# Laying weight panels out in DRAM as they lie in SBUF, in a four-layer diffusion trunk

## The chip, the core and the metric

The kernel runs on one core of a Trainium2 chip. The metric is the time of one execution on the device in microseconds (us), 1892.81 us for the kernel before (median of three runs). Engines are called PE (TensorE, matrix products), DVE (VectorE), ACT (ScalarE), POOL (GpSimd) and SP (SyncE, which only issues transfers here). Transfers between DRAM and the on-chip memory SBUF are done by 16 DMA engines, fed by queues: q1 is SP's, q10 is ACT's, q0 is POOL's.

## The reference

384 tokens of width 1024 (128 context, 256 latent) pass four layers. Each layer is a mixer and a mixture of experts, both modulated by vectors that come from `silu(cond) @ w_ada`:

```python
for i in range(DEPTH):                       # DEPTH = 4
    kind, j = i % 3, i // 3                  # 0 attention, 1 pooling, 2 retention
    mp = split(silu(c_ctx) @ w_ada[i] + b_ada[i], 6)      # w_ada: (4, 1024, 6144)
    ms = split(silu(c) @ w_ada[i] + b_ada[i], 6)
    h = rmsnorm(x) * norm1 * (1 + scale) + shift
    y = mixer(h)     # attn_w_qkv (1024, 1536), attn_w_o (1024, 1024); pool_w (4, 256, 256);
                     # ret_w_in (1024, 6144), ret_w_out (2048, 1024)
    x = x + gate * y
    h = rmsnorm(x) * norm2 * (1 + scale2) + shift2
    x = x + gate2 * moe(h)                   # 16 experts, two of them per token
y = rmsnorm(x) * norm_f
```

The retention mixer splits `h @ ret_w_in` into q and k (8 heads of 128), v and a gate (8 heads of 256), runs a forward and a backward scan over chunks of 128 tokens, and multiplies by `ret_w_out`. All values are float32.

## The kernel before

Weights of the mixers and of the modulation reach SBUF in **panels**: `panel` (line 112) is four buffers of 8 x 512 values per partition, 16 KB per partition, 2 MB each. A panel holds 1024 rows of a weight, row `k * 128 + p` at block k of partition p, and up to 512 columns. `load_panel` (line 307) issues it from SP; `panel_source` (314), `ret_qkv_source` (329) and `ret_gate_source` (334) say which part of the weight it is. The weights lie in DRAM as in the reference, so a partition's data is 8 pieces, one from each k, and the pieces are whole row parts:

- 64 modulation panels, 384 columns wide: 48 of them (layers 0 to 2) are loaded from line 372 (`load_ada`) before and during the attention of layer 0, alternating between panel buffers 2 and 3; 16 (layer 3) from line 380 (`load_ret_ada`) inside the retention loop. A piece is 1.5 KB.
- for each of the two attention layers (0 and 3) three panels of `attn_w_qkv` and two of `attn_w_o`, 512 columns wide, pieces of 2 KB.
- one pooling panel (layer 1), 256 columns wide in a 512-wide buffer.
- for each of the 8 heads of layer 2 a panel with q, k and v, put together by three transfers (pieces of 512 B, 512 B and 1 KB), and a gate panel of 256 columns (1 KB).
- four panels of `ret_w_out`, 512 columns wide: two for each half of the output columns.

All of these but the modulation panels alternate between buffers 0 and 1. A buffer is loaded again when PE has signalled that it has read it (`released`, line 244). For `ret_w_out` that is the end of a half of the output columns, after which the last two panels are loaded.

The experts' weights go through the same memory in other shapes (`load_half`, `load_down`, lines 343 to 350), in pieces of 4 KB; their layout is not touched.

**Between layers.** When PE has finished the experts of a layer it signals `experts_read` (line 1018), on which SP loads the first panels of the next layer (line 409): the pooling panel before layer 1; q/k/v and gate of head 0 and two modulation panels before layer 2; two `attn_w_qkv` panels before layer 3. In layers 1 and 3 the first experts' weights follow behind them in SP's queue. At the same time ACT stores the last experts' output rows to a DRAM table `y_by_slot`, and when they have landed POOL issues six indirect gathers (line 1857), two for each tile of 128 tokens, 128 rows of 4 KB each. ACT weights a landed pair (line 1800), DVE combines and gates it (lines 1472 and 1474), and POOL (first two tiles, line 1861) or DVE (last tile, line 1479) adds it to x. ACT squares and sums x, POOL takes the root, ACT scales x to `xn` (line 1568), and PE transposes it (line 512). PE has nothing else to do meanwhile.

In layer 0 PE weaves the modulation products (`pe_static_product`, line 552, matmuls at line 564) between the steps of the attention, one panel at a time. In layer 2 the loop over heads in `pe_retention` (line 723) does projections (lines 757 and 768), the scan, and two modulation products per head (line 541).

## Time and profile before

| | |
|---|---|
| median of 3 runs | 1892.81 us (1890.38 to 1894.35) |
| profiled execution | 1892.95 us, span 1890.8 us |
| PE busy | 1536.1 us, 81% |
| DVE, ACT, POOL busy | 521.1, 432.1, 130.9 us |
| mean granted PE clock | 0.911 of full speed |
| DMA | 196,042 packets, 436.91 MB, 231 GB/s over the span |
| SP's queue q1 | 179,504 packets, 392.75 MB, 56.7% of the 16 engines' time |

The profile is that of one execution. Its page gives busy times, groups of instructions by line, and counts by DMA queue. The list of waits tells how long an engine stood idle before an instruction and what released it; the timeline lists instructions with their start; the table by stage gives busy times, the granted clock, the share of time in which the 16 DMA engines were busy (it can pass 1, since the records of packets overlap a little) and what they moved. A share of the 16 engines' time divided by the number of packets gives what one packet takes of one engine. Packets of 4 bytes, with which transfers signal their end, are among the counts.

The busy share of the DMA engines is near 1 where the experts' weights are loaded and in the opening, 0.90 during most of layer 0's attention, and 0.46 in the retention loop.

### The profile page before, as it was taken

The page shows a single profiled execution, that of the slowest core. Times are in us where ns is not written, and L with a number is a line of the kernel's source. Part 1 is how long each engine was busy: PE and PEld are TensorE (multiplying, and loading weights), DVE is VectorE, ACT ScalarE, POOL GpSimd, SP SyncE. Part 2 cuts the span into 40 slices and gives each one's busy share as a digit, 9 for nine tenths or more (in the row PEclk, how much of TensorE's full clock was granted, in tenths as well). Part 3 has the DMA queues.
Part 4 walks back from the last instruction along what each step waited for, and adds up shares of the span by engine and source line. Part 5 has one row for each costly group of instructions (what it writes and reads, how often), then busy time and mean ns, then how long its engine had stood idle before and what let it go on. Part 6 is the DMA issues. An engine that isn't in the chain of part 4 may idle for free. (4 is left out here: it accounts for less than half of the span.)

```text
span 1890.8 us, 19158 instructions
## 1 busy us (share of the span) xinstructions
PE 1536.1 (81%) x7307; PEld 843.5 (45%) x7307; DVE 521.1 (28%) x1292; ACT 432.1 (23%) x836; POOL 130.9 (7%) x113
## 2 busy tenths in 40 slices
PE   5998779699835899299999998986997498969952
PEld 3445444444334444165555555434443347444421
DVE  0323100432037421332222222005410355063103
ACT  2114220312143111341111111003111306131211
POOL 0000001200023000200000000002000100110002
PEclk7999989899968899699999999897999699979976
DMA  9777886679863599634444444053897721039993
GB/s 358 246 274 254 309 305 211 266 298 411 329 258 111 210 412 398 214 104 148 147 144 144 144 146 165 0 222 134 330 412 305 291 89 51 0 134 380 412 364 112
DMA packets 196042, 436.91 MB, mean 231 GB/s; under 512 B 9552, under 2 KB 114800, under 8 KB 195824
## 3 DMA queue, kind: packets, MB, share of 16 engines
q1 hardware_dynamic: 179504, 392.75, 56.7%
q10 hardware_dynamic: 12992, 30.40, 4.3%
q0 software_dynamic: 3456, 12.58, 1.8%
q8 instruction: 54, 0.88, 0.2%
q14 instruction: 36, 0.29, 0.0%
HBM read 410.00 MB, written 25.69 MB: 230 GB/s over the span
## 5 line engine op out<-in xcount | busy, mean ns | idle before, releaser
L888 PE MATMUL bank<-gate_up_weights,hT_gathered 128*64 128x512 f32 (+1 forms) x1280 | 258.3, 605 | 23.4 <-SPq L478 20.0
L757 PE MATMUL bank<-panel,hT 128*128 128x512 f32 x384 | 170.5, 598 | 0.7 <-ACT mod_bc L1587 0.7
L888 PEld LDWEIGHTS bank<-gate_up_weights,hT_gathered 128*64 128x64 f32 (+1 forms) x1280 | 84.1, 134 | 189.7 <-issue 185.5
L512 PE MATMUL bank<-const_base,xn 128*128 128x128 f32 x192 | 39.3, 395 | 132.0 <-ACT xn L1568 132.0
L902 PE MATMUL bank<-down_weights,actT 128*64 128x512 f32 (+1 forms) x640 | 138.5, 603 | 2.3 <-ACT actT L1766 2.3
L584 PE MATMUL bank<-panel,hT 128*128 128x512 f32 x288 | 126.1, 595 | 1.1 <-DVE hT L1084 1.1
L564 PE MATMUL bank<-panel,cond_columns 128*32 128x384 f32 x768 | 86.6, 576 | 31.5 <-DMA panel<-in_w_ada 26.9
L757 PEld LDWEIGHTS bank<-panel,hT 128*128 128x128 f32 x384 | 71.2, 190 | 90.9 <-issue 90.1
L873 PE MATMUL bank<-h_hi,P 128*128 128x512 f32 x216 | 95.9, 444 | 9.8 <-DVE P L1417 9.8
L512 PEld LDWEIGHTS bank<-const_base,xn 128*128 128x128 f32 x192 | 37.1, 214 | 136.8 <-issue 115.1
L1593 ACT ACTIVATE ada_panel_rows<-bank 128x384 f32<-128x384 f32 x64 | 31.4, 490 | 270.8 <-PE bank L564 155.7
L873 PE MATMUL bank<-h_lo,P 128*128 128x512 f32 x216 | 88.9, 412 | 0.0
L584 PEld LDWEIGHTS bank<-panel,hT 128*128 128x128 f32 x288 | 53.9, 190 | 70.4 <-issue 69.1
L584 PE MATMUL bank<-panel,oT 128*128 128x512 f32 x192 | 84.2, 596 | 0.7 <-ACT oT L1673 0.7
L1456 DVE TENSOR_TENSOR act<-bank,silu 128x256 f32<-128x256 f32 x36 | 15.3, 424 | 251.5 <-ACT silu L1760 251.5
L768 PE MATMUL bank<-panel,hT 128*128 128x256 f32 x384 | 84.2, 379 | 0.0
L1099 DVE TENSOR_TENSOR residual_term<-bank,gate_bc 128x512 f32<-128x512 f32 x24 | 16.5, 691 | 229.3 <-PE bank L834 93.0
L768 PEld LDWEIGHTS bank<-panel,hT 128*128 128x128 f32 x384 | 72.4, 190 | 10.0 <-issue 0.5
L1771 ACT ACTIVATE y_rows<-bank 128x512 f32<-128x512 f32 x72 | 43.0, 597 | 139.6 <-PE bank L902 139.6
L1760 ACT ACTIVATE silu<-bank 128x256 f32<-128x256 f32 x36 | 13.8, 385 | 255.3 <-PE bank L888 255.3
L1857 POOL DMA_INDIRECT y_of_token<-y_by_slot,slot_of_token x24 | 22.9, 955 | 650.3 <-DMA y_by_slot<-y_rows 644.2
L873 PEld LDWEIGHTS bank<-h_hi,P 128*128 128x128 f32 x216 | 43.4, 201 | 43.7 <-issue 28.8
(269 smaller groups left out, 1999.7 us busy)
## 6 DMA issues: line engine op xcount, KB each, us to landing
panel<-in_w_ada SPq DMA_DIRECT2D x64, 1536.0 KB
down_weights<-in_moe_w_down SPq DMA_DIRECT2D x74, 1024.0 KB, 15.2
gate_up_weights<-in_moe_w_gate SPq DMA_DIRECT2D x148, 512.0 KB, 13.2
gate_up_weights<-in_moe_w_up SPq DMA_DIRECT2D x148, 512.0 KB, 14.2
y_by_slot<-y_rows ACTq DMA_DIRECT2D x36, 512.0 KB, 7.1
panel<-in_ret_w_in SPq DMA_DIRECT2D x16, 1024.0 KB
panel<-in_attn_w_qkv SPq DMA_DIRECT2D x6, 2048.0 KB
panel<-in_attn_w_o SPq DMA_DIRECT2D x4, 2048.0 KB
```

What stands on the lines that cost most here:

```text
L512: last = PE.transpose(ps[k % 4][:, t * 128:(t + 1) * 128], xn[:, t, k * 128:(k + 1) * 128], ident)
L564: last = PE.matmul(ps[7][32 * g:32 * g + 32, 0:ADA_N], cond32[:, 2 * g + kk, :], src[:, 2 * g + kk, 0:ADA_N], start=kk == 0, stop=kk == 1)
L584: last = PE.matmul(ps[bank][:], lhs(k, t), panel[s % 2][:, k, :], start=k == 0, stop=k == nk - 1)
L757: last = PE.matmul(ps[t][:], hT[:, k, t * 128:(t + 1) * 128], panel[f % 2][:, k, :], start=k == 0, stop=k == KD - 1)
L768: last = PE.matmul(ps[3 + t // 2][:, (t % 2) * 256:(t % 2) * 256 + 256], hT[:, k, t * 128:(t + 1) * 128], panel[(f + 1) % 2][:, k, 0:256], ...
L873: last = PE.matmul(ps[half][:], Pm[:, j, t, :], part[:, t, half * 512:half * 512 + 512], start=t == 0 and n == 0, stop=t == TILES - 1 and ...
L888: last = PE.matmul(ps[2][width * s:width * s + width, :], hg[:, j, k, width * s:width * s + width], gu_ring[w][:, :, k, :], start=k == 0, ...
L902: last = PE.matmul(ps[6 + half][width * s:width * s + width, :], actT[:, c, width * s:width * s + width], dn_ring[w][:, c, half * 512:half ...
L1099: V.tensor_tensor(tmp[:, m % 2, :], ps[3 * half + t][:], gate_bc[:, COND[t], half * 512:half * 512 + 512], ALU.mult).then_inc(sem("mix_ter ...
L1593: S.activation(mpan[:], ps[bank][:, 0:ADA_N], ACT.Copy).then_inc(sem("ada_evac"), 1)
L1771: S.activation(ybuf[:, par, half * 512:half * 512 + 512], ps[6 + half][:], ACT.Copy).then_inc(sem("row_y"), 1)
L1857: G.indirect_dma_start(ytok[:, a, t, :], None, y_rows[:], bass.IndirectOffsetOnAxis(slot_of_token[:, a, t:t + 1], 0)).then_inc(sem(f"y_gat ...
```

## The change

The host writes new arrays, in which every panel lies as its buffer does: for each of the 128 partitions the 8 pieces one behind the other (12 KB for a modulation panel, 16 KB for one of 512 columns, 8 KB for one of 256), and the partitions in order, so that a panel is one contiguous block of DRAM. The q, k and v columns of a retention head are put side by side, so that its panel is one transfer instead of three. The sources in the kernel are changed to these arrays. The buffers in SBUF, their number, the order of all transfers, the semaphores and what every engine computes stay the same. Modulation panels still fill 384 of the 512 columns of a buffer row, gate and pooling panels 256 of 512.

```diff
+def panel_layouts(inputs):
+
+    def columns(w, n):
+        *lead, rows, cols = w.shape
+        w = w.reshape(*lead, rows // 128, 128, cols // n, n)
+        w = np.moveaxis(w, (-2, -3, -4), (len(lead), len(lead) + 1, len(lead) + 2))
+        return np.ascontiguousarray(w).reshape(*lead, cols // n, 128, rows // 128 * n)
...
+    q, k, v, g = np.split(w["ret_w_in"][0], (RH * RK, 2 * RH * RK, 2 * RH * RK + RH * RV), axis=1)
+    heads = np.concatenate([q.reshape(D, RH, RK), k.reshape(D, RH, RK), v.reshape(D, RH, RV)], axis=2).reshape(D, RH * 512)
...
-    ada_w = A["w_ada"].rearrange("l (k p) n -> l p k n", p=128)
-    qkv_w = A["attn_w_qkv"].rearrange("l (k p) n -> l p k n", p=128)
...
+    ada_w, qkv_w, wo_w = A["ada_panels"], A["qkv_panels"], A["wo_panels"]
+    rin_w, rgate_w, rout_w, pool_w = A["ret_panels"], A["ret_gate_panels"], A["rout_panels"], A["pool_panels"]
...
+        rows = lambda w, n: w.rearrange("p (k n) -> p k n", n=n)
         if kind == "ada":
-            return lambda d: [(d[:, :, 0:ADA_N], ada_w[l, :, :, ds(i * ADA_N, ADA_N)])]
-        if kind == "attn" and not isinstance(i, int) or kind == "attn" and i < 3:
-            return lambda d: [(d[:, :, :], qkv_w[a, :, :, i * 512:(i + 1) * 512])]
+            src = ada_w[l, i] if isinstance(i, int) else ada_w[l, ds(i, 1)].rearrange("o p c -> (o p) c")
+            return lambda d: [(d[:, :, 0:ADA_N], rows(src, ADA_N))]
+        if kind == "attn" and i < 3:
+            return lambda d: [(d[:, :, :], rows(qkv_w[a, i], 512))]
...
     def ret_qkv_source(h):
-        return lambda d: [(d[:, :, 0:RK], rin_w[0, :, :, ds(h * RK, RK)]),
-                          (d[:, :, RK:2 * RK], rin_w[0, :, :, ds(h * RK + RH * RK, RK)]),
-                          (d[:, :, 2 * RK:512], rin_w[0, :, :, ds(h * RV + 2 * RH * RK, RV)])]
+        return lambda d: [(d[:, :, :], of_head(rin_w, h, 512))]
 
     def ret_gate_source(h):
-        return lambda d: [(d[:, :, 0:RV], rin_w[0, :, :, ds(h * RV + 2 * RH * RK + RH * RV, RV)])]
+        return lambda d: [(d[:, :, 0:RV], of_head(rgate_w, h, RV))]
```

## Rows read from the trace of the kernel before

**Rows 1.** Waits of PE, whole span: what waited, released by: us, times, longest us.
```profile
PE bank L512 <- ACT xn L1568: 132.0, 8, 36.4
PE bank L564 <- DMA panel<-in_w_ada: 26.9, 19, 2.7
```

**Rows 2.** Timeline, layer 2: first matmuls on the third `ret_w_out` panel.
```profile
1241.52 2.08 PE L834 MATMUL bank<-panel,yT_even 128*128 128x512 f32 x2 [7.98 <-DMA panel<-in_ret_w_out]
```

**Rows 3.** Waits of PE in 814 to 1190 us, the retention loop; the longest group.
```profile
PE bank L783 <- DVE ret_q_bwd L1238: 10.5, 8, 1.3
```

**Rows 4.** Table by stage: stretch, its us, engines busy; then PE clock, DMA share, GB/s.
```profile
28.00:34.00 6.00, 3.33 (x22) 1.69 (x22) 0.46 (x3) 2.83 (x6) 1.66 (x3) 0.50 1.06 373
180.00:288.00 108.00, 83.27 (x648) 49.40 (x639) 12.82 (x41) 26.84 (x70) 0.00 (x0) 0.87 0.90 310
665.00:705.00 40.00, 40.00 (x190) 18.16 (x188) 9.82 (x24) 9.06 (x18) 0.00 (x0) 1.00 1.03 412
766.00:769.00 3.00, 0.00 (x0) 0.00 (x0) 0.00 (x0) 0.00 (x0) 1.93 (x2) 0.50 1.03 292
814.00:1180.00 366.00, 339.48 (x1412) 210.21 (x1412) 85.03 (x242) 68.96 (x131) 6.56 (x8) 1.00 0.46 147
1480.00:1482.00 2.00, 0.00 (x0) 0.00 (x0) 1.33 (x1) 1.67 (x3) 2.00 (x1) 0.50 1.05 386
```

**Rows 5.** DMA queues (packets, MB, share): whole span; 817.5 to 823; 852 to 854.5.
```profile
q8 instruction: 54, 0.88, 0.2%
...
q10 hardware_dynamic: 148, 0.95, 41.3%
...
q10 hardware_dynamic: 158, 0.15, 17.3%
```

**Rows 6.** Waits of PE in 150 to 290 us, the attention of layer 0.
```profile
PE bank L564 <- DMA panel<-in_w_ada: 22.3, 15, 2.7
```

**Rows 7.** Timeline from layer 2 to layer 3: SP, POOL, ACT, DVE, PE.
```profile
1461.53 1.02 POOL L1857 DMA_INDIRECT y_of_token<-y_by_slot,slot_of_token  x1 [155.16 <-DMA y_by_slot<-y_rows]
1462.93 1.03 SPq L312 DMA_DIRECT2D panel<-in_attn_w_qkv  x2
1479.48 1.15 ACT L1800 ACTIVATE y_of_token<-y_of_token,route_scratch 128x1024 f32<-128x1024 f32 x1 [2.99 <-DMA y_of_token<-y_by_slot,slot_of_token]
1480.67 2.70 DVE L1472 SCALAR_TENSOR_TENSOR y_of_token<-y_of_token,route_scratch 128x1024 f32<-128x1024 f32 x1 [0.80 <-ACT y_of_token L1800]
1484.66 1.23 DVE L1479 TENSOR_TENSOR x<-x,y_of_token 128x1024 f32<-128x1024 f32 x1
1490.67 4.68 PE L512 MATMUL bank<-const_base,xn 128*128 128x128 f32 x24 [33.42 <-ACT xn L1568]
```

**Rows 8.** DMA queues in 529 to 534, 774 to 781.5, 1467.5 to 1478 us.
```profile
q1 hardware_dynamic: 287, 1.04, 51.5%
q0 software_dynamic: 287, 1.04, 51.3%
...
q0 software_dynamic: 634, 2.32, 77.9%
q1 hardware_dynamic: 677, 0.68, 25.8%
...
q0 software_dynamic: 694, 2.52, 60.4%
q1 hardware_dynamic: 857, 1.72, 42.8%
```

**Rows 9.** DMA queues in 1465.8 to 1467.5 us.
```profile
q1 hardware_dynamic: 278, 0.57, 88.7%
q0 software_dynamic: 25, 0.09, 14.7%
```

**Rows 10.** From layer 1 to layer 2: SP's issues, POOL's first gather; queue q0 in 766 to 771.
```profile
764.05 4.72 SPq L312 DMA_DIRECT2D panel<-in_ret_w_in  x4
766.62 0.99 POOL L1857 DMA_INDIRECT y_of_token<-y_by_slot,slot_of_token  x1 [155.27 <-DMA y_by_slot<-y_rows]
...
q0 software_dynamic: 4, 0.02, 0.9%
```

More of the change, by code:

```diff
@@ L85, in shape_constants @@
     return {"k_base": base, "k_ret": ret, "k_rope": rope, "k_cnt": (np.float32(1) / cnt)}
+def panel_layouts(inputs):
[4 more added lines that the diff above has]
+        return np.ascontiguousarray(w).reshape(*lead, cols // n, 128, rows // 128 * n)
+    w = {n: np.asarray(inputs[n]) for n in ("w_ada", "attn_w_qkv", "attn_w_o", "pool_w", "ret_w_in", "ret_w_out")}
+    q, k, v, g = np.split(w["ret_w_in"][0], (RH * RK, 2 * RH * RK, 2 * RH * RK + RH * RV), axis=1)
+    heads = np.concatenate([q.reshape(D, RH, RK), k.reshape(D, RH, RK), v.reshape(D, RH, RV)], axis=2).reshape(D, RH * 512)
+    out = columns(w["ret_w_out"][0].reshape(2, D, D), 512)
+    pools = w["pool_w"].reshape(-1, KD, 128, 256).transpose(0, 2, 1, 3).reshape(-1, 128, KD * 256)
+    return {"ada_panels": columns(w["w_ada"], ADA_N), "qkv_panels": columns(w["attn_w_qkv"], 512), "wo_panels": columns(w["attn_w_o"], 512),
+            "ret_panels": columns(heads, 512), "ret_gate_panels": columns(g, RV), "pool_panels": np.ascontiguousarray(pools),
+            "rout_panels": np.ascontiguousarray(out.transpose(1, 0, 2, 3)).reshape(4, 128, KD * 512)}
 def build_trunk(nc, A, O, depth=DEPTH):
@@ L259, in panel_landed @@
         eng.wait_ge(sem(f"panel_landed{s % 2}"), 48 * (s // 2 + 1) + i * (48 * per // 2))
-    ada_w = A["w_ada"].rearrange("l (k p) n -> l p k n", p=128)
-    qkv_w = A["attn_w_qkv"].rearrange("l (k p) n -> l p k n", p=128)
-    wo_w = A["attn_w_o"].rearrange("l (k p) n -> l p k n", p=128)
-    rin_w = A["ret_w_in"].rearrange("l (k p) n -> l p k n", p=128)
-    rout_w = A["ret_w_out"].rearrange("l (k p) n -> l p k n", p=128)
+    ada_w, qkv_w, wo_w = A["ada_panels"], A["qkv_panels"], A["wo_panels"]
+    rin_w, rgate_w, rout_w, pool_w = A["ret_panels"], A["ret_gate_panels"], A["rout_panels"], A["pool_panels"]
     wg_w = A["moe_w_gate"].rearrange("l e (p k) f -> l e p k f", p=128)
@@ L315, in panel_source, with of_head @@
         a = l // 3
+        rows = lambda w, n: w.rearrange("p (k n) -> p k n", n=n)
         if kind == "ada":
[L317 to L319 removed]
+            src = ada_w[l, i] if isinstance(i, int) else ada_w[l, ds(i, 1)].rearrange("o p c -> (o p) c")
+            return lambda d: [(d[:, :, 0:ADA_N], rows(src, ADA_N))]
+        if kind == "attn" and i < 3:
+            return lambda d: [(d[:, :, :], rows(qkv_w[a, i], 512))]
         if kind == "attn":
[L321 removed]
+            return lambda d: [(d[:, :, :], rows(wo_w[a, i - 3], 512))]
         if kind == "pool":
[L323 to L324 removed]
+            return lambda d: [(d[:, :, 0:256], rows(pool_w[a], 256))]
         if kind == "rout":
[L326 removed]
+            return lambda d: [(d[:, :, :], rows(rout_w[i], 512))]
         raise ValueError(kind)
+    def of_head(w, h, n):
+        src = w[h] if isinstance(h, int) else w[ds(h, 1)].rearrange("o p c -> (o p) c")
+        return src.rearrange("p (k n) -> p k n", n=n)
     def ret_qkv_source(h):
[L330 to L332 removed]
+        return lambda d: [(d[:, :, :], of_head(rin_w, h, 512))]
     def ret_gate_source(h):
[L335 removed]
+        return lambda d: [(d[:, :, 0:RV], of_head(rgate_w, h, RV))]
     def at_e(w, l, e):
@@ L1893, in build_trunk @@
     ctx.close()
-_INS = ["x_prompt", "x_sample", "cache_k", "cache_v", "state_ret", "w_ada", "b_ada", "attn_w_qkv", "attn_q_norm",
-        "attn_k_norm", "attn_w_o", "pool_w", "ret_w_in", "ret_decay_logit", "ret_norm", "ret_w_out",
+_INS = ["x_prompt", "x_sample", "cache_k", "cache_v", "state_ret", "b_ada", "attn_q_norm",
+        "attn_k_norm", "ret_decay_logit", "ret_norm",
         "moe_w_gate", "moe_w_up", "moe_w_down"]
@@ L1917 @@
     arrays["router"] = np.concatenate([weights.reshape(128, -1), np.broadcast_to(bias, (128, bias.size))], axis=1).astype(np.float32)
+    arrays.update(panel_layouts(inputs))
     arrays.update(shape_constants())
```

4 lines of the change are left out of this document (removed).

## The prediction, made before the changed kernel ran

> **What bounds the kernel now.** I read the page first: TensorE (PE) is busy for 81% of the span, so the question is what ends its idle time, and whether a panel is ever the last thing to arrive. The waits of PE answer it [rows 1]. The largest item, 132.0 us in 8 waits, is PE standing idle at the norms until ScalarE has written `xn`; between layers that is the combine of the experts' outputs (store to DRAM, gather back by token, weight, add), not a panel. Panels from `w_ada` end 26.9 us in 19 waits, and one panel of `ret_w_out` ends one of 7.98 us [rows 2]; no other panel ends any. Inside the retention loop no wait is put down to a DMA; the longest group waits for DVE, 10.5 us in 8 [rows 3]. So of the 95 panels only the modulation panels of layer 0 and one output panel of layer 2 can give time by landing sooner.
>
> Then I asked what a panel costs the 16 DMA engines. Stretches in which one packet size has the engines to itself give the rate: runs of 1.5 KB move 373 GB/s, of 2 KB 386, of 4 KB 412, and the retention panels (512 B and 1 KB mixed) 292 [rows 4]. Per engine (16 x bytes / rate) that is 65.9 ns for 1.5 KB, 84.9 for 2 KB and 159 for 4 KB. The last two give a line of 10.8 ns + 36.2 ns per KB; it puts 1.5 KB at 65 ns, so a packet pays a fixed 11 ns and the rest is bytes. No stretch shows a separate toll for scattered rows: 1.5 KB rows fetched 24 KB apart lie on the line of the experts' 4 KB runs. That is why I expect nothing from locality itself. The Trainium skill (DMA: Bandwidth & Descriptors, section on latency and other measured facts) warns that DRAM row pitches of large powers of two can halve the rate, and the old `ret_w_out` and `attn_w_o` panels do step by 512 KB from one k to the next. [...]
>
> **What the change does to each panel.** I count a packet as long as the shorter of its two contiguous runs, in DRAM and in SBUF. Panels that fill a 512-wide buffer (`attn_w_qkv`, `attn_w_o`, `ret_w_out`, the q, k, v of a head) become contiguous on both sides: 128 packets of 16 KB in place of 1024 of 2 KB, or 3072 of 512 B and 1 KB. Packets above 4 KB do exist unsplit: the instruction queue has 54 in 0.88 MB, 16 KB each, and the 8 KB rows of `ret_norm` take 313 ns of an engine each (0.413 x 5.5 us x 16 / 116, the line gives 301) [rows 5]. By the line a 16 KB packet takes 604 ns, 434 GB/s; 412 GB/s is the lower bound. The modulation (1.5 KB of a 2 KB row), gate and pooling panels (1 KB of 2 KB) are still written in short pieces in SBUF. The nearest row for a transfer whose one side is longer than the other is the store of `ret_state_out`: 2 KB contiguous in SBUF, 1 KB runs in DRAM. It shows 158 packets for 0.15 MB, so 1 KB each, at about 48 ns, no cheaper than a 1 KB packet on the line (47) [rows 5]. I take it that these panels keep their packets and their price.
>
> **Part 1, modulation panels of layer 0: 0 us.** In 180 to 288 us the DMA engines are 90% busy [rows 4], with 1.5 KB packets, and from 150 to 290 PE waits 22.3 us for panels in 15 waits [rows 6]. This is the place where faster panels would pay. With the packets unchanged it pays nothing. Bounds: no loss, since the experts' weights, contiguous by partition like the new panels, run at 412 GB/s [rows 4]; at the other end the gain of the second rival below.
>
> **Part 2, the output panel of layer 2: -0.5 us.** SyncE may issue the third `ret_w_out` panel only when half 0 is done, and PE resumes at 1241.52 after 7.98 us [rows 2]. 2.10 MB at 386 GB/s are 5.43 us, at 434 GB/s 4.83, at 412 5.09: 0.3 to 0.6 saved, the latency stays. Behind it PE has three tiles of 16 matmuls before it needs the fourth panel, so nothing else is late.
>
> **Part 3, retention and attention panels elsewhere: 0 us.** Their landings are covered: PE waits for DVE and ACT in the loop [rows 3], where the DMA engines are 46% busy [rows 4]. SyncE issues one transfer per head where it issued three; its queue holds nothing that PE awaits. What their cover costs if it is gone: one landing, 5 us, at each head.
>
> **Part 4, the gather between layers 2 and 3: +5.9 us.** Here a panel costs time without anyone waiting for it. GpSimd issues six gathers of 512 KB from 1461.53, and SyncE, released by the same end of the experts, issues two `attn_w_qkv` panels (4.19 MB) from 1462.93 [rows 7]. Both use the same 16 engines, the gathers as queue q0, SyncE's loads as q1. How these are shared shows where the two queues run side by side, in counts: 287 packets against 287 when both are 4 KB, 634 against 677 when the other side is 1 KB, 694 against 857 at 2 KB [rows 8] (4-byte ones included). So the engines alternate packet by packet, whatever their size. With 1 or 2 KB opposite, the gather had two thirds or more; with 16 KB opposite it has 4 of 20. Worked out: from 1467.5 to 1478 the gather moves its last 2.52 of 3.15 MB [rows 8], in the 1.7 us before 0.09 (a gap in which q1 has the engines) [rows 9], so 0.54 by 1465.8. After the change q1 has about 0.9 MB through at 1467.5 (1.7 us at 434 GB/s and the little before), which leaves 3.3 MB or 202 packets of 16 KB. A pair, 604 + 159 ns, over 16 engines is 21 pairs per us: 9.6 us, to 1477.1, in which the gather moves 202 x 4 KB = 0.83 MB and stands at 1.44 of 3.15. The rest goes against the experts' 4 KB packets at the measured 1.04 MB per 5 us: 8.2 us, to 1485.3 instead of 1478, +7.3. The path behind it: the third weighting (L1800) would start at 1486.8 instead of 1479.48; then 1.15 + 1.28 + 1.22 + 1.23 us and hand-overs bring the last add to 1491.8, against 1485.89. Before, L1472 took 2.70 beside GpSimd's add [rows 7]; a later one has no such neighbour, which returns 1.4. PE's norm waits for exactly this chain: +5.9. Bounds: 0 if the gather's share does not fall, +7.8 if the panels drain first (third rival).
>
> **Part 5, the same between layers 1 and 2: +0.5 us.** SyncE issues at 764.05, GpSimd at 766.62, and the gather's data starts only after 771 (0.02 MB in 766 to 771) [rows 10]. 2.10 MB in 16 KB packets from about 766 are through at 771; then come gate and modulation panels, as before. 0 to 1.8 us (three packets of 604 ns ahead of a late store or a first gather packet); I take 0.5, near the lower end since the overlap is nearly nil. Between layers 0 and 1 the pooling panel keeps 1 KB packets: 0.
>
> **Sum.** 0 - 0.5 + 0 + 5.9 + 0.5 = +5.9 us. The profiled execution lasted 1892.95 us, its span 1890.8; the median of three is 1892.81, 0.14 less. 1892.81 + 5.9 = **1898.7 us**.
>
> **Rivals.** First, *no difference*: 16 KB runs are cut into pieces of about 4 KB, or the engines alternate in smaller units than what the trace calls a packet. Then the gather has half: 2.52 MB at 0.208 MB per us are 12.1 us instead of 10.5, so at most +1.6. Against it: the unsplit 8 KB rows. Result 1892.3 to 1894.5. That covers also a change that does not do what it says.
>
> Second, *faster*: the price of a packet sits on the DRAM side. Then a modulation panel, now read in 12 KB runs, costs 3.82 us (412 GB/s) instead of 4.22, 0.40 less. In 15 waits that is 6.0 us, with the opening's six panels 2.4 more; the granted clock in 180 to 288 is 0.87 after these pauses and 1.00 in the retention loop [rows 4], and of the 83.3 us that PE is busy there up to 0.13 x 83.3 = 10.8 could go, of which I count 6 at most. Gain 8.4 to 14.4, less the 5.9 of the sum: 1884.3 to 1890.3, centre 1887. It wins from about 15 cheaper panels on. For it: the two sides of a transfer may well be cut separately; the Trainium skill (same page, section on semaphore increments) mentions loads on this chip whose reads are widened over several rows. Against it: the state store.
>
> Third, *worse*: in 1465.8 to 1467.5 the gather got 25 packets against 278 [rows 9]. If this is a backlog that drains first, all 16 KB packets go first, to 1475.0, then 2.54 MB at 0.208 MB per us: 1487.2, +7.8 on the path, and 1.8 at the boundary before: 1901.9.
>
> **Numbers.** Forecast 0.45, no difference 0.17, faster panels 0.25, drained first 0.10, other 0.03. The range from 1884 to 1902 leaves out the lower tail of the second rival and the upper of the third. A difference of 0.2% (3.8 us) is about what can be told from none. Slower: 0.40 of the forecast's 0.45, plus the third: 0.50. Same: 0.05 + 0.17 + 0.09 (where gain and loss cancel): 0.31. Faster: 0.16 + 0.03: 0.19.
>
> **What would show it.** In the profile after: fewer packets in all, about 196,000 less 36,000; 1.5 KB stretches still at 373 GB/s (rival two: 400 or more); in the gather before layer 3 about as many q0 as q1 packets, and the idle time of PE ahead of L512 there 39 us instead of 33.4; the wait for `ret_w_out` 7.5 us. The prediction is wrong if SyncE issues the layer 3 panels some us earlier than the gather, as it does before layer 2, since most of their bytes would then be gone before the two meet.

## The result, and the profile of the changed kernel

The changed kernel took 1906.03 us (median of 4 runs, 1901.09 to 1907.83), the kernel before 1893.58 us beside it: a ratio of 1.0064, 95% interval 1.0044 to 1.0083, so it is slower by 12.5 us. The direction is as forecast, and so is one place of the loss, the gather before layer 3. The size is not: +5.9 us were predicted, and the time lies above the upper end of the range (1902). A second set of runs of the same kernel on another chip gave a ratio of 1.0107 (1.0078 to 1.0136).

The page of the changed kernel (packets in all; then the queues, with packets, MB and share of 16 engines):

```profile
DMA packets 159690, 436.91 MB, mean 230 GB/s; under 512 B 9296, under 2 KB 89968, under 8 KB 156656
...
q1 hardware_dynamic: 143152, 392.75, 56.1%
q10 hardware_dynamic: 12992, 30.40, 4.2%
q0 software_dynamic: 3456, 12.58, 1.8%
```

The waits of PE over the whole span (released by: us, times, longest us):

```profile
PE bank L530 <- ACT xn L1586: 137.2, 8, 40.2
PE bank L582 <- DMA panel<-in_ada_panels: 27.3, 18, 3.6
PE bank L801 <- DVE ret_q_bwd L1256: 10.5, 8, 1.3
PE bank L852 <- DMA panel<-in_rout_panels: 7.8, 1, 7.8
PE bank L906 <- DMA gate_up_weights<-in_moe_w_up: 5.6, 5, 1.7
```

L530 is the old L512, L582 the old L564, L801 the old L783, L852 the old L834 and L906 the old L888. Against [rows 1] the idle time before the norms has grown by 5.2 us, and its longest piece from 36.4 to 40.2. The waits for modulation panels are where they were (26.9 before). The last line has no counterpart in the kernel before: PE now waits for the experts' weights, which the change does not touch. That line is the first trace of what the prediction missed.

The table by stage (stretch, its us, engines busy, then PE clock, DMA share, GB/s):

```profile
28.00:34.00 6.00, 3.33 (x19) 1.91 (x22) 0.46 (x3) 3.06 (x6) 1.65 (x3) 0.50 1.06 373
180.00:288.00 108.00, 83.61 (x632) 51.31 (x631) 12.82 (x41) 27.28 (x70) 0.00 (x0) 0.86 0.90 306
665.00:705.00 40.00, 40.00 (x192) 18.17 (x188) 9.82 (x24) 8.99 (x18) 0.00 (x0) 1.00 1.02 404
814.00:1180.00 366.00, 339.34 (x1413) 209.98 (x1412) 84.66 (x240) 69.75 (x132) 5.96 (x7) 1.00 0.43 147
```

Beside [rows 4]: the 1.5 KB stretch still runs at 373 GB/s, the attention of layer 0 still has the DMA engines about 90% busy (306 GB/s where it had 310), and in the retention loop PE is as busy as before, with the DMA engines at 43% instead of 46%. The experts' stretch, 665 to 705, has gone from 412 to 404 GB/s at a nearly unchanged share of busy engines (1.02 and 1.03).

To see where the time went I cut both profiled executions at three marks in each layer: GpSimd's first `h_lo` (the router), GpSimd's first gather, and PE's first matmul of the next norm. Times in us:

| stretch | before | after | difference |
|---|---|---|---|
| start to layer 0's router | 359.2 | 356.6 | -2.6 |
| experts, layers 0, 1, 2 | 160.6, 161.0, 160.7 | 164.4, 164.0, 165.0 | +11.1 |
| gather to norm, layers 0 to 1, 1 to 2 | 32.0, 29.6 | 31.5, 28.7 | -1.4 |
| gather to norm, layers 2 to 3 | 29.1 | 35.8 | +6.7 |
| mixer of layer 1 | 53.8 | 53.3 | -0.5 |
| mixer of layer 2 | 504.6 | 500.5 | -4.1 |
| mixer, experts and end of layer 3 | 400.1 | 399.2 | -0.9 |

The sum is +8.3, against +8.1 between the spans of 1898.9 and 1890.8 us (the marks are rounded). This profiled execution, 1901.09 us, is the fastest of the four. Mixer 2 is 500 to 506 us long in the runs below, old layout or new, so I read nothing into its 4 us. Two items remain: the gather before layer 3, as forecast, and the experts' stages, which no term of the sum had.

The gather before layer 3. Timeline from layer 2 to layer 3:

```profile
1463.81 1.02 POOL L1875 DMA_INDIRECT y_of_token<-y_by_slot,slot_of_token  x1 [159.31 <-DMA y_by_slot<-y_rows]
1464.93 2.85 SPq L327 DMA_DIRECT2D panel<-in_qkv_panels  x2
...
1476.78 1.15 ACT L1818 ACTIVATE y_of_token<-y_of_token,route_scratch 128x1024 f32<-128x1024 f32 x1 [16.73 <-DMA y_of_token<-y_by_slot,slot_of_token]
...
1484.80 1.15 ACT L1818 ACTIVATE y_of_token<-y_of_token,route_scratch 128x1024 f32<-128x1024 f32 x1 [6.87 <-DMA y_of_token<-y_by_slot,slot_of_token]
...
1489.86 1.15 ACT L1818 ACTIVATE y_of_token<-y_of_token,route_scratch 128x1024 f32<-128x1024 f32 x1 [3.92 <-DMA y_of_token<-y_by_slot,slot_of_token]
...
1499.63 0.66 PE L530 MATMUL bank<-const_base,xn 128*128 128x128 f32 x2 [40.24 <-ACT xn L1586]
```

The queues in 1469.8 to 1480.3 us (packets, MB, share), the stretch that lies as far behind the first gather as the last one of [rows 8]:

```profile
q1 hardware_dynamic: 270, 3.35, 75.2%
q0 software_dynamic: 269, 1.02, 23.7%
```

270 packets against 269, with q1's panels in 16 KB packets and q0 in 4 KB ones: one for one, so the gather moves 1.02 MB where it had moved 2.52 [rows 8]. The third weighting starts 26.05 us after the first gather; it was 17.95 [rows 7].

The experts. The end of layer 0's experts on PE in the changed kernel:

```profile
500.04 3.64 PE L906 MATMUL bank<-gate_up_weights,hT_gathered 128*32 128x512 f32 x32
505.41 3.64 PE L906 MATMUL bank<-gate_up_weights,hT_gathered 128*32 128x512 f32 x32 [1.74 <-DMA gate_up_weights<-in_moe_w_up]
510.02 0.44 PE L912 MATMUL bank<-const_base,act 128*128 128x128 f32 x2 [0.97 <-DVE act L1474]
511.33 5.34 PE L920 MATMUL bank<-down_weights,actT 128*32 128x512 f32 x32 [0.88 <-ACT actT L1784]
```

and the same in the kernel before:

```profile
502.88 7.07 PE L888 MATMUL bank<-gate_up_weights,hT_gathered 128*32 128x512 f32 x64
510.92 0.44 PE L894 MATMUL bank<-const_base,act 128*128 128x128 f32 x2 [0.96 <-DVE act L1456]
511.83 3.64 PE L902 MATMUL bank<-down_weights,actT 128*32 128x512 f32 x32 [0.47 <-ACT actT L1766]
```

Before, the 64 gate and up matmuls ran through. After, PE stops for 1.74 us in the middle for an `in_moe_w_up` half, and the 32 down matmuls behind the pause then take 5.34 us instead of 3.64. The granted clock of 500 to 518 us is 0.91 in the changed kernel, so part of it ran at the lower level of 1.2 GHz (511 to 514 us, right behind the two pauses, has 0.58), and 1.00, 2.4 GHz throughout, in the kernel before. The changed kernel's row:

```profile
500.00:518.00 18.00, 13.06 (x98) 3.86 (x98) 0.42 (x1) 2.55 (x5) 0.00 (x0) 0.91 0.42 164
```

So this late weight was paid twice. The cause of the lateness had to be sought. While the experts' weights are loaded the DMA engines are fully busy in both kernels (665 to 705 us above), and the change edits none of these loads. What it does change for them is where their arrays stand in the order in which the inputs are declared. The change replaces six arrays ahead of the experts' three by seven behind them.

### The profile page after: what moved, and what is told of

It reads as the page before. It is cut to its first block and busy times, and to the rows that moved or that the text cites. A ratio compares the mean times of both kernels' runs of the same rounds, so it can differ in the third digit from the quotient of the medians.

```text
span 1898.9 us, 19114 instructions
## 1 busy us (share of the span) xinstructions
PE 1529.6 (81%) x7307; PEld 837.6 (44%) x7307; DVE 519.0 (27%) x1292; ACT 430.8 (23%) x836; POOL 131.3 (7%) x113
## 5 line engine op out<-in xcount | busy, mean ns | idle before, releaser
L906 PE MATMUL bank<-gate_up_weights,hT_gathered 128*64 128x512 f32 (+1 forms) x1280 | 256.4, 599 | 30.3 <-SPq L496 21.3
L906 PEld LDWEIGHTS bank<-gate_up_weights,hT_gathered 128*64 128x64 f32 (+1 forms) x1280 | 83.3, 132 | 195.7 <-issue 181.9
L530 PE MATMUL bank<-const_base,xn 128*128 128x128 f32 x192 | 36.1, 372 | 137.2 <-ACT xn L1586 137.2
L582 PE MATMUL bank<-panel,cond_columns 128*32 128x384 f32 x768 | 84.9, 566 | 31.7 <-DMA panel<-in_ada_panels 27.3
L891 PE MATMUL bank<-h_hi,P 128*128 128x512 f32 x216 | 95.3, 441 | 11.1 <-DVE P L1435 11.1
L530 PEld LDWEIGHTS bank<-const_base,xn 128*128 128x128 f32 x192 | 33.9, 201 | 142.4 <-issue 120.2
L920 PEld LDWEIGHTS bank<-down_weights,actT 128*64 128x64 f32 (+1 forms) x640 | 36.3, 134 | 65.2 <-issue 57.3
## 6 DMA issues: line engine op xcount, KB each, us to landing
gate_up_weights<-in_moe_w_gate SPq DMA_DIRECT2D x148, 512.0 KB, 13.6
gate_up_weights<-in_moe_w_up SPq DMA_DIRECT2D x148, 512.0 KB, 14.9
```

The costliest lines, as they stand in the source:

```text
L530: last = PE.transpose(ps[k % 4][:, t * 128:(t + 1) * 128], xn[:, t, k * 128:(k + 1) * 128], ident)
L582: last = PE.matmul(ps[7][32 * g:32 * g + 32, 0:ADA_N], cond32[:, 2 * g + kk, :], src[:, 2 * g + kk, 0:ADA_N], start=kk == 0, stop=kk == 1)
L891: last = PE.matmul(ps[half][:], Pm[:, j, t, :], part[:, t, half * 512:half * 512 + 512], start=t == 0 and n == 0, stop=t == TILES - 1 and ...
L906: last = PE.matmul(ps[2][width * s:width * s + width, :], hg[:, j, k, width * s:width * s + width], gu_ring[w][:, :, k, :], start=k == 0, ...
L920: last = PE.matmul(ps[6 + half][width * s:width * s + width, :], actT[:, c, width * s:width * s + width], dn_ring[w][:, c, half * 512:half ...
```

## Experiments

"Stages" are the experts' stretches of layers 0 to 2 as cut above, "gaps" the three stretches from gather to norm. Times in the verdicts are medians; each ratio is to the kernel before on the same chip.

**Theories.** G: the gather is starved by 16 KB packets, and this is all. P: the order of the arrays costs something by itself. L: the new panels themselves slow later loads. The first four runs separate them.

**The order alone.** The kernel before, with the six arrays declared behind the others:

```diff
+    for n in ("w_ada", "attn_w_qkv", "attn_w_o", "ret_w_in", "pool_w", "ret_w_out"):
+        arrays[n] = arrays.pop(n)
     arrays.update(shape_constants())
```

> The kernel before, with its old layouts, but the six weight arrays declared last among the DRAM inputs, where the changed kernel has its panel arrays (same sizes). Theory P (the order of the arrays in DRAM slows the experts' weight loads, which cost 3 to 4 us in each of the first three layers of the changed kernel): 1899 us or more against 1893, with pauses of PE for gate_up weights in the last row of each layer. Theory G (only the 16 KB packets opposite the gather cost time) and theory L (the new panels themselves slow later loads): 1893, within 2 us.

Measured: 1897.28 us, ratio 1.0038 (1.0019 to 1.0057); stages 164.3, 162.7, 162.3; gap before layer 3 28.6. Three waits of PE for `in_moe_w_up`, 1.8 us. Not one transfer is different, and 7 us are lost; the three stages together are 7.0 us longer. Theory G alone falls.

**The changed kernel in the old order.** The seven new arrays take the places of the six old ones:

```diff
+    order = ["x_prompt", "x_sample", "cache_k", "cache_v", "state_ret", "ada_panels", "b_ada", "qkv_panels", ..., "moe_w_gate", "moe_w_up", "moe_w_down", "vectors", "router"]
+    arrays = {n: arrays[n] for n in order + [n for n in arrays if n not in order]}
```

> The changed kernel, with its arrays declared in the order of the kernel before, so that the experts' weights stand where they stood. Theory P: 6 us less than the changed kernel, near 1899, and PE waits of L906 for gate_up weights gone. Theories G and L: 1905, as the changed kernel.

Measured: 1898.82 us, ratio 1.0057 (1.0038 to 1.0075). Stages 160.3, 161.1, 161.2, no wait for the experts' weights, gap before layer 3 35.9. The experts' loss is cured with all the new panels in place, so theory L falls; the gather's stays. But the time is still 10.8 us above the kernel before (7.2 to 14.2), 4 to 5 us more than the gather explains, and the start to the first router takes 364.4 us, where the kernel before has 359.2.

**Two panels alone.** The kernel before with only the first two `attn_w_qkv` panels of layer 3 laid out by the host, in an array behind all others:

```diff
+        if kind == "attn" and l == 3 and i < 2:
+            return lambda d: [(d[:, :, :], A["two_panels"][i].rearrange("p (k n) -> p k n", n=512))]
```

> The kernel before, with only the first two attn_w_qkv panels of layer 3 contiguous (16 KB packets), as one further array at the end. Theory G: PE's idle time before the norm of layer 3 rises from 33.4 to 39 to 41 us and the time by 6 to 7 us, to 1899.5. If the 16 KB packets do not matter there: 1893 and 33.4 us.

Measured: 1893.95 us, ratio 1.0029 (1.0007 to 1.005), 5.5 us. PE's idle time before the norm of layer 3 is 40.3 us and the gap 36.0, the changed kernel's values, from 2 of 95 panels. Stages 160.3, 160.9, 160.2.

**Those two undone.** The changed kernel, with these two panels read from the old layout (a copy of it at the end of the arrays):

```diff
+        if kind == "attn" and l == 3 and i < 2:
+            return lambda d: [(d[:, :, :], A["attn_w_qkv"].rearrange("l (k p) n -> l p k n", p=128)[a, :, :, i * 512:(i + 1) * 512])]
```

> The changed kernel, with only these two panels of layer 3 loaded in the old layout (2 KB packets) from a copy of the old array at the end. Theory G: the idle time before the norm of layer 3 is back to 33 to 34 us and the time 6 to 7 us below the changed kernel, near 1899; what then remains over 1893 is not the gather's. If the gather is not the cause: 1905.

Measured: 1900.02 us, ratio 1.0058 (1.0037 to 1.0079). Gap 28.8, idle time 33.5: the gather's loss is gone, yet the kernel is still 11 us slower than the one before (7.0 to 14.9), hardly less than the changed kernel itself. The waits for the experts' weights are there (1.3 us in 2), and the stages are 161.1, 162.4 and 163.0, 4.2 us more than before in sum. The start to the first router is long again, 365.5 us.

**The changed kernel again**, on the chip of the next three:

> The changed kernel again, unchanged, beside the others of this group. Gather (about +7) and array order (about +7) together: 12 to 14 us over the kernel before. In its trace the gap from the first gather to the norm of layer 3 is 36 us and each of the first three experts' stages 162 to 165 us, against 29 and 161 before.

Measured: 1909.93 us, ratio 1.0107 (1.0078 to 1.0136); gap before layer 3 35.4, three waits for `in_moe_w_up`, 3.1 us. Stages 161.0, 161.8, 164.6: only the third is as long as was expected, so the loss by the order varies from one execution to the next.

**The gather has the engines to itself.** The kernel before, with SyncE held back until the gathers of the layer have landed:

```diff
                 sp.wait_ge(sem("experts_read"), l)
+                for t in range(TILES):
+                    sp.wait_ge(sem(f"y_gathered{t}"), 32 * l)
```

> The kernel before, but SyncE waits for the six gathers of a layer before it issues the next layer's first panels, so that the gather has the DMA engines to itself. If sharing the engines is what makes the gather long even with 2 KB packets: the gap from the first gather to the norm falls from 32.0, 29.6 and 29.1 us to about 24 each (alone, at the end of the kernel, the third pair is weighted 12.8 us after the first gather, against 17 to 22 in the middle), so 15 to 20 us less in all, near 1872 where the kernel before has 1889. If the loads, now 10 to 13 us late, are then waited for, the gain is given back: PE would pause for panels or gate_up weights.

Measured: 1879.51 us, ratio 0.9939 (0.9918 to 0.9959). Timeline before layer 3:

```profile
1457.36 1.02 POOL L1859 DMA_INDIRECT y_of_token<-y_by_slot,slot_of_token  x1 [155.36 <-DMA y_by_slot<-y_rows]
...
1469.88 1.15 ACT L1802 ACTIVATE y_of_token<-y_of_token,route_scratch 128x1024 f32<-128x1024 f32 x1 [1.66 <-DMA y_of_token<-y_by_slot,slot_of_token]
1470.03 1.03 SPq L312 DMA_DIRECT2D panel<-in_attn_w_qkv  x2
```

The third weighting starts 12.5 us after the first gather, where the kernel before has 17.95 and the changed one 26.05. The three gaps are 25.9, 25.8 and 25.4 us, 13.6 less in sum; mixer 1 gives 1.9 back because its panels come later (55.7 in place of 53.8). The difference, 11.7, agrees with the gain measured, 11 us, though the profiled execution is the slowest of the nine (span 1882.9 against 1890.8, with 2.5 us more in the start). The gather was being slowed before the change too, only less.

**Shorter packets' price.** The kernel before, where only the modulation panels are laid out by the host and are packed in their SBUF buffer as well, so that both sides of the transfer are runs of 12 KB (the matmuls read the packed view):

```diff
+            whole = lambda d: d[:].rearrange("p k n -> p (k n)")[:, 0:KD * ADA_N]
+            return lambda d: [(whole(d), src)]
```

> The kernel before, with only the modulation panels laid out by the host, and also packed in their SBUF buffers (8 x 384 values without gaps), so that both sides are contiguous: 128 packets of 12 KB per panel. If the short run in SBUF is what kept the packets of the changed kernel at 1.5 KB: 57,000 packets fewer, a panel costs about 3.6 us of the engines instead of 4.2, and PE's waits for modulation panels (27 us) fall to 15 to 20, the time by 6 to 12 us. If the packet price does not matter there: 1889, as before.

Measured: 1885.67 us, ratio 0.9978 (0.9954 to 1.0002), 4 us, an interval that just includes no gain. The page and the table by stage:

```profile
DMA packets 138698, 436.91 MB, mean 232 GB/s; under 512 B 9552, under 2 KB 49264, under 8 KB 130288
...
28.00:34.00 6.00, 3.81 (x26) 1.50 (x30) 0.15 (x1) 1.09 (x3) 0.93 (x2) 0.63 0.98 394
```

57,344 packets fewer from 64 panels, and the opening runs at 394 GB/s instead of 373. In the changed kernel the same panels, contiguous in DRAM, kept their 1.5 KB packets and the 373 GB/s. So in these transfers a packet is as long as the shorter run of the two sides.

**The experts' arrays first of all**, in the kernel before (six arrays and the small ones behind them):

> The kernel before, with the three arrays of experts' weights declared first among the DRAM inputs and nothing else changed. If the order of the old kernel was a lucky one and most others are slower: experts' stages of 162 to 165 us and 1893 to 1897. If only the new order is unlucky: 161 us each and 1889.

Measured: 1888.34 us, ratio 0.999 (0.9974 to 1.0005), stages 160.4, 160.7, 161.5. It is not that the experts' arrays begin early in DRAM.

**The wait in the changed kernel.** The three lines of the gather's wait added to it, order of arrays as changed:

> The changed kernel, whole, in its own order of arrays, with SyncE held back until the gathers of the layer before have landed, so that no 16 KB packet meets a gather. If the gather's starvation is worth what the idle of PE before the norms shows (40 us before layer 3 down to 30, 36 and 33 down to 30 before layers 1 and 2, 19 us in all): about 1890 to 1893, that is 0 to +3 us against the kernel before, since what the order of the arrays costs (5 to 7 us) and the longer experts' stages stay. Rival, the late panels are now waited for: the norms' idle falls but PE waits for the first qkv and modulation panels afterwards, 5 us each, and the time stays at 1900 or more. Second rival, the starvation explains all of the change's cost and the array order nothing: 1880, like the kernel before with the same wait.

Measured: 1891.66 us, ratio 1.0019 (1.0002 to 1.0035); gaps 25.7, 25.6, 26.5; stages 162.2, 165.4, 162.1; four waits for `in_moe_w_up`, 2.8 us. The gather's part is gone, and what the stages lose is the order's. The total does not close: the order's 7 to 9 us less the 11 us of the wait would be 2 to 4 us faster than the kernel before, and it is 3.6 slower.

**All layouts, old order, packed modulation panels, and the wait** (the changed kernel with all three edits):

> All of the host layouts, the arrays declared in the order of the kernel before, the modulation panels packed in their buffer too (12 KB packets), and SyncE held back until the gathers have landed. If the costs of the change are the gather's starvation and the array order and nothing else, both are gone: as fast as the kernel before with the same wait (11 us under the kernel before) and the 0 to 5 us of the packed modulation panels on top: 1875 to 1881. If there is a third cost of the 16 KB packets (in the experts' stages or in the retention layer), it shows as a time above 1881, with experts' stages above 161 us or the stage of mixer 2 above 505 us.

Measured: 1872.83 us, ratio 0.9921 (0.99 to 0.9942); stages 160.1, 161.0, 160.8; start to router 353.2.

**Packed modulation panels and the wait alone**, every other panel and array as before:

> The kernel before with two edits: modulation panels laid out by the host and packed in their buffer (12 KB packets), and SyncE held back until the gathers have landed. No other panel is changed, no array moved. The two gains add if they are separate (11 and 4 us): 1875 to 1880. Against the run with all panels laid out: equal if 16 KB packets of the other panels neither help nor harm once the gather is alone; below it if they harm elsewhere; above it by up to 2 us if the retention and attention panels gain. Only the 11 us if the packed modulation panels bring nothing: 1880 to 1882.

Measured: 1872.97 us, ratio 0.9921 (0.9903 to 0.9938); start to router 351.1. Both are 15 us faster than the kernel before and equal to each other within their intervals of some 4 us: no gain or harm of the attention, output, retention and pooling layouts is seen once the gather is alone and the order is the old one. The gains of the wait (11 us) and of the packed panels (4 us) add up to what is measured; the times themselves lie below the ones expected because the kernel before took 1887.71 us on this chip.

**The order alone, again**, with more runs:

> The kernel before with the six weight arrays declared last, the same as in the earlier run, in more rounds, because the earlier interval (+3.6 to +10.8 us) rests on few runs. If the order of arrays in DRAM costs time by itself: +4 to +10 us again, experts' stages of layers 0 to 2 at 162 to 164 us in place of 161, and waits of PE in the gate/up lines put down to DMA. If the earlier result was a difference between loadings of a program and not of the order: within 3 us of the kernel before, experts' stages 160 to 161.

Measured: 1896.17 us, ratio 1.0041 (1.0026 to 1.0056), stages 162.7, 164.9, 162.6.

**Which array's place?** In the kernel before, `w_ada` alone last:

> The kernel before with only w_ada (101 MB) declared last. If it is w_ada's place behind the experts' arrays that costs time (its panels are fetched beside the experts' weights in every layer): +5 to +9 us, experts' stages of layers 0 to 2 at 162 to 165 us. If it is the place of the other five, or only where the experts' arrays begin when all six are gone: within 3 us, stages at 160 to 161.

Measured: 1887.25 us, ratio 0.9996 (0.9984 to 1.0008), stages 160.4, 161.1, 161.4. The other five last:

> The kernel before with the five other weight arrays (attn_w_qkv, attn_w_o, ret_w_in, pool_w, ret_w_out; 56 MB) declared last and w_ada in place. If w_ada's place is the cause: within 3 us of the kernel before. If any shift of the experts' arrays to a start that differs from the old one costs time: +5 to +9 us.

Measured: 1897.22 us, ratio 1.0046 (1.0027 to 1.0066), stages 164.6, 164.4, 162.2. All six last, and the experts' arrays first of all:

> The kernel before with the six arrays last and the experts' arrays first of all: as in the run with the six last, w_ada lies behind the experts' arrays, but the 4.3 MB of small arrays (x, caches, state, b_ada) lie between them. If what costs is that w_ada lies behind the experts' arrays: +5 to +9 us. If it is the experts' start behind the 4.3 MB of small arrays: within 3 us, as in the run with the experts' arrays first.

Measured: 1888.31 us, ratio 1.0001 (0.9984 to 1.0018), stages 160.2, 161.0, 160.2. Neither `w_ada`'s place nor the amount of weight ahead of the experts decides. If the arrays lie one behind the other as declared, the experts' arrays begin at 153 MiB in the kernel before, at 57 with `w_ada` last and at 0 when first, none of which costs; at 4 MiB with the six last and at 100 with the five last, which cost (all but the 0 plus the same 0.1 MiB of small arrays). The costly ones are even, the harmless ones odd or exactly 0, and the only one of the six whose size is an odd number of MiB is `pool_w`, 1 MiB. This gave the last pair.

**`pool_w` alone last:**

```diff
+    for n in ("pool_w",):
+        arrays[n] = arrays.pop(n)
```

> The kernel before with pool_w alone (1.05 MB, the smallest weight array) declared last, so that everything declared after it moves by 1 MiB, the experts' arrays with it. If an odd shift of the experts' arrays by 1 MiB is what costs: +6 to +9 us, experts' stages of layers 0 to 2 at 162 to 165 us, from moving one small array. If the amount of weight ahead of the experts' arrays, or the place of one of the large ones (qkv, o, ret_w_in, ret_w_out), is what costs: within 3 us, stages at 160 to 161.

Measured: 1898.85 us, ratio 1.0046 (1.003 to 1.0062), stages 161.2, 162.6, 162.8, two waits for `in_moe_w_up`. The sum of the stages is 4.3 us above the kernel before, and so is the span of this execution, the fastest of the twelve.

**All but `pool_w` last:**

> The kernel before with five weight arrays (w_ada, qkv, o, ret_w_in, ret_w_out; 155 MB) declared last and pool_w left in its place. It moves almost all that the costly order moves, but the experts' arrays by an even number of MiB (148). If the shift by 1 MiB costs: within 3 us of the kernel before, stages at 160 to 161. If the place of the large arrays costs: +6 to +9 us.

Measured: 1892.43 us, ratio 1.0006 (0.999 to 1.0023), stages 160.1, 161.0, 162.2. The table by stage for 1730 to 1790 us (layer 3's experts), `pool_w` last:

```profile
1730.00:1790.00 60.00, 60.00 (x286) 26.52 (x284) 14.00 (x36) 12.20 (x24) 0.00 (x0) 1.00 1.02 402
```

and all but `pool_w` last:

```profile
1730.00:1790.00 60.00, 60.00 (x286) 26.49 (x284) 12.23 (x30) 12.21 (x24) 0.00 (x0) 1.00 1.02 411
```

To move one array of 1 MiB, which is read in 1 of 95 panels, costs 8 us; to move 148 MiB and leave that one costs nothing that can be measured. (In layer 3, whose experts' stretch from router to gather is longer, 184 us, the lower rate costs no time: it is 184.1 in both.) What the DMA engines show is more slow packets. The usual 4 KB packet takes 159 ns; those over 200 ns, counted from router to gather in all four layers, are 1635 with `pool_w` last, 1308 with all but `pool_w` last and 1148 in the kernel before. Over all twenty traces of this study, the twelve in which the experts' arrays begin at an odd MiB or at 0 have 1045 to 1308 such packets, and the eight in which they begin at an even one 1405 to 1651. A short stretch does not separate them so well: in 390 to 500 us it is 115 to 237 against 261 to 320, but in 1725 to 1795 us 14 to 120 against 99 to 192, which overlap.

**The order in the changed kernel**, with the gather's wait, to be set beside the same kernel in the new order (1.0019):

> The changed kernel with SyncE held back until the gathers have landed and its arrays declared in the old order; the run in the new order was 4 us slower than the kernel before (1.0019). If the order costs 7 us in the changed kernel too: 3 to 4 us faster than the kernel before, or more, up to 11 faster (the whole gain of the wait), with experts' stages at 161 us. If the order costs nothing in the changed kernel: +4 us again. The packed modulation panels of the fastest runs are not in this one, so what it lacks of -15 us is theirs.

Measured: 1886.73 us, ratio 0.9984 (0.9968 to 1.0), stages 160.4, 160.6, 160.8, no wait for the experts' weights. The order is worth 0.35%, some 7 us, here too.

This kernel and the one with all layouts (0.9921) differ in one thing, whether the modulation panels are packed in their buffer. That is 12 us, each taken against the kernel before on its own chip, and in the profiled executions the start to the first router alone is longer by that much, 365.8 against 353.2 us (spans 1883.5 and 1873.5). In the kernel before, laying out and packing the same panels gave 4 us together. So laid out and not packed, as the change has them, they seem to cost some 8 us against the old layout. No run has them alone, so this is a difference of ratios and not shown by itself.

## Why the prediction was right about the gather and wrong in its sum

The step that failed is the sum. It has no term for the experts' stages, which is to put them at 0 without a reason, and the runs showed 7 to 9 us there, from the order of the arrays alone. The gather's mechanism held and its term was about right. Variants of the changed kernel show a further loss of 2 to 9 us, whose cause stays open.

**Part 1, modulation panels: 0 forecast, borne out by the profiled execution, not by all runs.** 15 waits of 23.0 us in 150 to 290 us against 22.3 [rows 6], and packets and the rate of the opening are unchanged, as taken from the shorter run. But in three of six kernels with these panels the start is 5 to 7 us longer than in the kernel before (see what stays open), so 0 may be wrong. The second rival (the price sits on the DRAM side) is refuted by the unchanged 373 GB/s and, from the other side, by the packed run, where the SBUF side alone made the difference. Its gain was sized too high: with really cheaper packets the start is 6 to 8 us shorter and the whole 4 us (at most 9), where the rival had 8.4 to 14.4 before taking off the gather; it reckoned with 412 GB/s and the packed panels run at 394.

**Part 2, the output panel: -0.5 forecast, -0.1 measured** (7.98 to 7.84 us). Over all traces the wait is 7.75 to 8.12 us with the old panel and 7.59 to 8.17 with the new one, so no gain can be told. The price of a 16 KB packet was about right: in the middle of the two panels, 1235 to 1242 us of the changed kernel and 1235.5 to 1240.5 of the kernel before,

```profile
DMA packets 199, 3.00 MB, mean 428 GB/s; under 512 B 16, under 2 KB 16, under 8 KB 16
...
DMA packets 953, 1.95 MB, mean 390 GB/s; under 512 B 0, under 2 KB 0, under 8 KB 953
```

But from the first packet to the end of the last the two panels take 11.3 us where they took 11.8, half of what was forecast for each. The second line also mends a reading. The 386 GB/s [rows 4] of the prediction belongs to the two `attn_w_qkv` panels, which step by 768 KB from one k to the next; these are `ret_w_out` panels, which do step by 512 KB, and they run as fast. And the line of the prediction is per 1000 bytes: it gives 66 ns for 1.5 KB and 307 for 8 KB, where the text has 65 and 301; no term moves by it.

**Part 3, covered panels: 0, right.** The loop's longest wait is 10.5 us in 8 as in [rows 3]. The two runs at 0.9921 agree for all these panels together, to within their intervals.

**Part 4, the gather before layer 3: +5.9 forecast, +6.8 of PE's idle time measured** (33.42 to 40.24), 6.7 in the gap. The mechanism was right to the count of packets (269 and 270): 15.6 us behind the first gather it had moved 1.38 MB, where the working has 1.44 at 1477.1. Some of the 0.9 us that it fell short lies at the start: SyncE issued 1.12 us behind the first gather instead of 1.40 [rows 7], and in 1468.1 to 1469.8 us the gather still had only 12 packets against 42:

```profile
q1 hardware_dynamic: 42, 0.69, 95.9%
q0 software_dynamic: 12, 0.05, 6.6%
```

That is the gap of [rows 9], which the working had taken from the trace before; the third rival's backlog beyond it was not there, and one-for-one held after it. A slip without weight: beside 2 KB packets the gather had 59% of the bytes (2.52 of 4.24 MB [rows 8]) and not two thirds or more. The Trainium skill (DMA: Bandwidth & Descriptors, section on queues, rings and completion order) says that each engine takes a whole packet from one queue before it turns to the next, and puts a packet at 9 to 17 descriptors. The turn-taking is what this trace shows; in what the trace lists as packets, the turn is worth one entry, be it 4 or 16 KB.

**Part 5, the boundary before layer 2: +0.5 forecast, nothing measured.** The idle time before this norm went from 34.21 to 33.04 us, but the trace before is at the long end of its kind: over the kernels with the old panels of layer 2 and without the added wait of SyncE it is 32.8 to 34.2, with the new ones 32.4 to 33.1. SyncE's issues of the two retention panels were over at 768.50, where four had taken it 4.72 us [rows 10], and the first gather came at 769.7, so the two hardly met.

**The term that was missing: the order of the arrays, 7 to 9 us.** The prediction followed each transfer that the change edits and none that it does not. Two things that lay open should have led there. The diff takes six names out of `_INS` and appends the new arrays behind the experts' and the small ones, so it moves the experts' arrays in the order of declaration. And the experts' stage was read only as a price list: 412 GB/s at a share of 1.03, with PE busy 40.00 of 40 us [rows 4]. Both resources are full there, so a loss of 1 to 2% of the rate comes out as time, and PE's pauses take the clock with them. That 1 MiB decides could not be read from the trace; that this stage has no slack could, and it would have been a rival with a price: 2% of three stages of 161 us is 10 us.

**The sum that the runs give:** gather 5.5 (two panels alone, 1.3 to 9.4; 6.7 by its gap) and order 7 to 9 (four runs of the kernel before, 1.0038 to 1.0046), 13 to 16 us. The changed kernel measured 12.5 and, on the other chip, 20 us. Taking the parts out again does not close the account. With the order restored 10.8 us are left where 5 to 7 should be, with the two panels undone 11 where 7 to 9 should be. With the wait the changed kernel is 6 to 8 us slower than its parts say (1.0019), and with the old order as well 8.5 us slower than the kernel before with the same wait (0.9984 against 0.9939).

**What stays open.** First, why the 1 MiB decides. The rule "even MiB costs, odd or 0 does not" fits nine orders of which two were tried to test it; that the arrays lie as declared is an assumption, and whether it is their own address or the distance to other arrays wasn't tried. The Trainium skill (DMA: Bandwidth & Descriptors, section on latency and other measured facts) tells of row pitches from one partition to the next at large powers of two, in copies between DRAM arrays; it takes channel aliasing for the cause, as an inference, and even there a pitch of 512 KiB has 207 GB/s where the full rate is 214. Here all rows and pitches are equal in both orders and only a start moves, which that rule does not cover. Second, the 2 to 9 us above. They appear in all four variants in which the modulation panels are laid out but not packed and in the changed kernel's second set, not in its first, and they are gone where the panels are packed. In profiled executions three of six such kernels took 364 to 366 us to the first router, where the old layout takes 356 to 362 in eleven; the other three, the changed kernel's own two among them, took 357 to 360. What makes the start longer, and only in some, isn't settled: PE's waits for the panels are no longer in two of the three (23.0 and 27.5 us against 26.9; 34.9 in the third). The missing run is these panels alone, laid out and not packed. Third, the two sets of runs of the changed kernel differ by 7 us, and their intervals hardly overlap.

## What to carry to other kernels

A longer packet is not free for the others: the queues took turns by packet here, so before a bulk load gets 16 KB packets, look for the small transfer on another queue that the next stage waits for, and hold the load back until it has landed; here that alone was worth 11 us, more than any layout. Lay a source out contiguously only together with its destination, since the shorter run set the packet here, and doing it on one side alone may have cost time. And when the host's arrays change in number or order, the stages that are at the DMA limit have to be looked at even if none of their lines has changed: take them as a term of the sum, and try the old order.

## What the runs showed of the hardware that was not expected

The order in which the inputs are declared moves the time by 0.4% with not one instruction changed: stages of 161 us become 161 to 165, with the count of 4 KB packets over 200 ns in the four experts' stages going from 1045 to 1308 up to 1405 to 1651. A packet of 12 KB in a stretch alone runs at 394 GB/s where 1.5 KB pieces have 373, and 16 KB packets run at 428 where 2 KB ones have 390; yet beside a gather of 4 KB packets the 16 KB ones cost the kernel 5.5 us. And a pause of 1.74 us for a weight was followed by a second loss of 1.70 us in the 32 down matmuls behind it, at a granted clock of 0.91 over 18 us in place of 1.00.
